# The causal mask of the first attention, added by GpSimd to each head's forget sums

## The reference

```python
def forgetting_attention(q, k, v, log_f):          # 16 heads of 64, Q_BLOCK = 128
    scale = dh ** -0.5
    c = jnp.cumsum(log_f.astype(jnp.float32), axis=1).transpose(0, 2, 1)
    for i in range(S // Q_BLOCK):
        q0 = i * Q_BLOCK
        q1 = q0 + Q_BLOCK
        s = jnp.einsum("bqhd,bkhd->bhqk", q[:, q0:q1], k[:, :q1]).astype(jnp.float32) * scale
        s = s + c[:, :, q0:q1, None] - c[:, :, None, :q1]
        causal = jnp.arange(q0, q1)[:, None] >= jnp.arange(q1)[None, :]
        p = jax.nn.softmax(jnp.where(causal, s, -jnp.inf), axis=-1)
        outs.append(jnp.einsum("bhqk,bkhd->bqhd", p.astype(v.dtype), v[:, :q1]))
```

## Time and profile before

| | |
|---|---|
| median of 3 runs | 2632.52 us (2631.8 to 2633.27) |
| the profiled execution, its own time | 2633.66 us |
| its span in the profile | 2631.9 us, mean granted clock 0.997 |
| PE busy | 2607.0 us, 99% of the span |
| DVE / ACT / POOL busy | 1370.2 / 968.8 / 123.8 us |
| scores of the first attention begin (L565) | 132.4 us |
| its last transposes and products end, inside `aout` | about 228 us |

### The profile page before, as it was taken

How to read it: one execution, slowest core, us unless ns; L and a number is a source line. 1 busy time by engine, 2 the same in 40 slices (tenths; PEclk the granted TensorE clock), 3 DMA queues, 4 the chain that set the end, 5 groups by cost and what they waited for, 6 DMA issues and landing times.

```text
span 2631.9 us, 30728 instructions
## 1 busy us (share of the span) xinstructions
PE 2607.0 (99%) x12322; PEld 2121.4 (81%) x12322; DVE 1370.2 (52%) x2142; ACT 968.8 (37%) x1528; POOL 123.8 (5%) x138
## 2 busy tenths in 40 slices
PE   9999999999999999999998999999999999999999
PEld 7867888888888788888875788888888688888887
DVE  4365763664434776376657544344542365544343
ACT  4265442443226643244445432233223233432221
POOL 0000000000001100000012000000120500000000
PEclk9999999999999999999999999999999999999999
DMA  4311233232232133223320233233332032323222
GB/s 154 126 64 56 90 96 104 96 104 97 96 104 65 43 104 111 81 96 104 95 90 26 73 104 104 86 99 96 104 121 88 9 104 96 97 96 104 91 99 83
DMA packets 66830, 240.49 MB, mean 91 GB/s; under 512 B 7728, under 2 KB 7856, under 8 KB 66560
## 3 DMA queue, kind: packets, MB, share of 16 engines
q1 hardware_dynamic: 63936, 229.38, 26.6%
q0 software_dynamic: 2752, 9.15, 1.1%
HBM read 236.37 MB, written 2.13 MB: 91 GB/s over the span
## 4 chain that ended last, share of the span: by engine, by line
PE 95%; DVE 2%; ACT 2%; issue 1%; POOL 0%; DMA 0%; SPq 0%; DVEq 0%; POOLq 0%; ACTq 0%
PE ps L453 29%; PE ps L454 29%; PE ps L455 29%; PE ps L565 2%; PE ps L585 1%; PE ps L605 1%; PE ps L857 1%; ACT m_B_P L1745 1%; PE ps L844 1%; ACT m_E_P L1745 0%; PE ps L518 0%; PE ps L571 0%; DMA m_x<-in_xT 0%; DVE m_E_P L1018 0%; PE ps L521 0%
## 5 line engine op out<-in xcount | busy, mean ns | idle before, releaser
L453 PE MATMUL ps<-m_xs,m_wsp 128*128 128x512 f32 x2232 | 873.8, 391 | 3.2 <-DVE m_xs L929 3.2
L455 PE MATMUL ps<-m_xs,m_wsp 128*128 128x512 f32 x2232 | 869.1, 389 | 0.0
L454 PE MATMUL ps<-m_xs,m_wsp 128*128 128x512 f32 x2232 | 869.0, 389 | 0.0
L1636 ACT ACTIVATE m_wsp<-m_raw 128x1024 fp32r<-128x1024 f32 (+1 forms) x429 | 446.0, 1051 | 783.3 <-PE ps L455 750.5
L902 DVE TENSOR_TENSOR m_wsp<-m_raw,m_wsp 128x1024 fp32r<-128x1024 f32 (+1 forms) x429 | 516.8, 1221 | 162.6 <-ACT m_wsp L1636 162.3
L453 PEld LDWEIGHTS ps<-m_xs,m_wsp 128*128 128x128 f32 x2232 | 419.4, 188 | 92.5 <-issue 6.1
L454 PEld LDWEIGHTS ps<-m_xs,m_wsp 128*128 128x128 f32 x2232 | 419.5, 188 | 88.0 <-issue 1.7
L455 PEld LDWEIGHTS ps<-m_xs,m_wsp 128*128 128x128 f32 x2232 | 419.4, 188 | 87.2
L955 DVE TENSOR_TENSOR m_x<-m_x,ps 128x512 f32<-128x512 f32 x104 | 71.0, 687 | 316.6 <-PE ps L455 316.6
L453 PE MATMUL ps<-m_wsp,m_xs 128*128 128x512 f32 x320 | 125.7, 393 | 0.0
L455 PE MATMUL ps<-m_wsp,m_xs 128*128 128x512 f32 x320 | 125.1, 391 | 0.0
(11 more groups left out here) (301 smaller groups left out, 3181.8 us busy)
## 6 DMA issues: line engine op xcount, KB each, us to landing
m_raw<-in_w SPq DMA_DIRECT2D x427, 512.0 KB, 3.3
m_A_cb<-csum POOLq DMA_DIRECT2D x16, 256.0 KB, 3.8
m_x<-in_xT SPq DMA_DIRECT2D x4, 512.0 KB, 7.8
m_B_bias<-in_biasB POOLq DMA_DIRECT2D x8, 256.0 KB, 3.1
out<-m_x SPq DMA_DIRECT2D x8, 256.0 KB, 2.0
m_raw<-in_w SPq DMA_DIRECT2D x4, 256.0 KB, 6.9
m_O_D<-in_decay POOLq DMA_DIRECT2D x1, 1024.0 KB, 5.0
m_O_cs<-in_ropeo POOLq DMA_DIRECT2D x1, 512.0 KB, 4.7
```

What stands on the lines that cost most here:

```text
L453: e.matmul(out, lh, rh, start=first, stop=False)
L454: e.matmul(out, lh, rl, start=False, stop=False)
L455: return e.matmul(out, ll, rh, start=False, stop=final)
L1636: e.activation(wsp[n % NSP][:, 0, o:1024], raw[n % NRAW][:, o:1024], ACT.Copy).then_inc(*s_hi(n))
```

## The change

On PE the mask products are gone. In their place the mask is in the row that DVE adds. A buffer of `A_cb` is now 7 blocks of 128 columns wide: the loaded sums stand in blocks 3 to 6, GpSimd adds the fp32 `mask` to copies of key blocks 0, 1 and 2 in blocks 0 to 2, and to key block 3 in place, in block 6. It does this for each of the 16 heads with two instructions (`A_masked`), and DVE's `scored` waits for it (`s_masked`) and no longer for the load itself.

For each query block the masked keys must lie beside plain ones in a way that one instruction of DVE can read. So the key blocks stand in another order: (1, 0) for query block 1, (2, 0, 1) for query block 2. The scores of these two blocks therefore take two products instead of one, first the masked block and then the others. DVE reads the 2 blocks of query block 1 with a step between them. The values are taken in the new order (`kbs`).

```diff
-def causal_units(pairs):
+def causal_units(pairs, orders=((0,), (0, 1), (0, 1, 2), (0, 1, 2, 3))):
...
-            A_cb = ring(c, "A_cb", 6, [128, S])
...
+            A_cb = ring(c, "A_cb", 6, [128, 7 * 128])
...
-                        last = {}
-                        for j in u.jobs:
-                            s = j.segs[si]
-                            last[j] = e.matmul(bank(pre, "score", j.n)[:, s["c0"]:s["c0"] + s["n"]], spec["q"](u, j, s),
-                                               spec["k"](u, j, s), start=True, stop=not spec["more"](j, s))
-                        for j in u.jobs:
-                            s = j.segs[si]
-                            more = spec["more"](j, s)
-                            for ei, (o, n, lt, rh) in enumerate(more):
-                                last[j] = e.matmul(bank(pre, "score", j.n)[:, s["c0"] + o:s["c0"] + o + n], lt, rh,
-                                                   start=False, stop=ei == len(more) - 1)
-                            if s is j.segs[-1]:
+                        for part in zip(*(spec["k"](u, j, j.segs[si]) for j in u.jobs)):
+                            last = {}
+                            for j, (o, n, keys) in zip(u.jobs, part):
+                                s = j.segs[si]
+                                last[j] = e.matmul(bank(pre, "score", j.n)[:, s["c0"] + o:s["c0"] + o + n],
+                                                   spec["q"](u, j, s), keys, start=True, stop=True)
...
-                k=lambda u, j, s: A_k[64 * j.par:64 * j.par + 64, u.p, 0:s["n"]],
-                more=lambda j, s: [(s["n"] - 128, 128, identb[:, :], maskb[:, :])],
+                k=A_keys,
...
-                biased=lambda u, j: d_cb[j.h % 6]["cb", j.h]))
...
+                P=A_P, st=A_st, among=nothing, out=out_split("A"), bias=A_bias, biased=lambda u, j: s_masked[j.h]))
...
-            for h in range(16):
+            def A_sums(h):
                 if h >= 6:
                     q.wait_ge(*s_top["A", A_units[3 * ((h - 6) // 2) + 2].jobs[-1].n])
-                load(A_cb[h % 6][:, :], a["csum"][h:h + 1, :].broadcast_to([128, S]), d_cb[h % 6], ("cb", h))
+                load(A_cb[h % 6][:, 384:896], a["csum"][h:h + 1, :].broadcast_to([128, S]), d_cb[h % 6], ("cb", h))
+
+            def A_masked(h):
+                cb = A_cb[h % 6]
+                q.wait_ge(*d_mk["mk"])
+                q.wait_ge(*d_cb[h % 6]["cb", h])
+                three, one = (mask[:, :].rearrange("p (b n) -> p b n", b=1).broadcast_to([128, 3, 128]), mask[:, :])
+                e.tensor_tensor(cb[:, 0:384].rearrange("p (b n) -> p b n", b=3),
+                                cb[:, 384:768].rearrange("p (b n) -> p b n", b=3), three, ALU.add)
+                e.tensor_tensor(cb[:, 768:896], cb[:, 768:896], one, ALU.add).then_inc(*s_masked(h))
+
+            for h in range(6):
+                A_sums(h)
+            for h in range(16):
+                A_masked(h)
+                if h % 2 and h < 11:
+                    A_sums(h + 5)
+                    A_sums(h + 6)
```

More of the change, by code:

```diff
@@ L9 @@
 F32R = mybir.dt.float32r
-BF16 = mybir.dt.bfloat16
-U16 = mybir.dt.uint16
 ALU = mybir.AluOpType
@@ L198, in causal_units @@
                     n = 128 * (qb + 1)
-                    segs.append(dict(c0=c0, n=n, qb=qb, kbs=range(qb + 1), oc=128 * qb))
+                    segs.append(dict(c0=c0, n=n, qb=qb, kbs=orders[qb], oc=128 * qb))
                     c0 += n
@@ L267, in build @@
         ident = sb(ctx, "ident", [128, 128])
-        identb = sb(ctx, "identb", [128, 128], BF16)
-        maskb = sb(ctx, "maskb", [128, 128], BF16)
+        mask = sb(ctx, "mask", [128, 128])
         ones = sb(ctx, "ones", [128, 128])
@@ L397, in bank @@
             return ps[bank_of.get(key, 0)]
-        d_cf, d_id, d_idb, d_mk = (sem(f"d_{n}", 16) for n in ("cf", "id", "idb", "mk"))
+        d_cf, d_id, d_mk = (sem(f"d_{n}", 16) for n in ("cf", "id", "mk"))
         d_x = [sem(f"d_x{i}", 16) for i in range(4)]
@@ L1016, in scored @@
                             sc = bank(pre, "score", j.n)[:, s["c0"]:s["c0"] + s["n"]]
+                            to = P[j.n % len(P)][:, s["c0"]:s["c0"] + s["n"]]
+                            if pre == "A" and s["qb"] == 1:
+                                sc, to = (t.rearrange("p (b n) -> p b n", b=2) for t in (sc, to))
                             q.wait_ge(*spec["biased"](u, j))
                             i = e.tensor_tensor_reduce(
-                                out=P[j.n % len(P)][:, s["c0"]:s["c0"] + s["n"]], in0=sc, in1=spec["bias"](u, j, s),
+                                out=to, in0=sc, in1=spec["bias"](u, j, s),
                                 scale=-1.0, scalar=3.0e38, op0=ALU.add, op1=ALU.min, accum_out=mx[:, si:si + 1])
@@ L1162, in vector_program, with A_bias @@
             over(ST["ain"], ain)
+            def A_bias(u, j, s):
+                cb = A_cb[j.h % 6]
+                if s["qb"] == 1:
+                    return cb[:, 128:640].rearrange("p (b t n) -> p b t n", b=2, t=2)[:, :, 0, :]
+                return cb[:, {0: slice(0, 128), 2: slice(256, 640), 3: slice(384, 896)}[s["qb"]]]
             scored, loop = attention("A", A_units, dict(
-                P=A_P, st=A_st, among=nothing, out=out_split("A"), bias=lambda u, j, s: A_cb[j.h % 6][:, 0:s["n"]],
-                biased=lambda u, j: d_cb[j.h % 6]["cb", j.h]))
+                P=A_P, st=A_st, among=nothing, out=out_split("A"), bias=A_bias, biased=lambda u, j: s_masked[j.h]))
             over(ST["av"], rows_out(ST["av"], A_v, rc("mix0"), s_col["mix0"]),
@@ L2107, in gpsimd_program @@
             load(ident[:, :], a["ident"], d_id, "id")
-            load(identb[:, :].bitcast(U16), a["identb"], d_idb, "idb")
-            load(maskb[:, :].bitcast(U16), a["maskb"], d_mk, "mk")
+            load(mask[:, :], a["mask"], d_mk, "mk")
             e.memset(A_onr[:, :], 1.0).then_inc(*s_zero("A"))
@@ L2271, in host_consts @@
     o = {}
-    def bits(v):
-        return (np.ascontiguousarray(v).view(np.uint32) >> 16).astype(np.uint16)
     o["ident"] = np.eye(128, dtype=f)
-    o["identb"] = bits(np.eye(128, dtype=f))
     i = np.arange(128)
-    o["maskb"] = bits(np.where(i[:, None] >= i[None, :], 0.0, NEG).astype(f))
+    o["mask"] = np.where(i[:, None] >= i[None, :], 0.0, NEG).astype(f)
     m = np.zeros((128, S), f)
```

28 lines of the change are left out of this document (18 added, 10 removed).

## The result

After the change the median is 2645.41 us (four runs, 2644.66 to 2649.98), beside 2632.19 us for the kernel before (four runs). The medians differ by 13.2 us. The ratio, taken over all runs, is 1.0053, 95% interval 1.0037 to 1.0069: slower by 13.9 us, at least 9.7. The forecast said about 2641 us, between 2636.0 and 2645.5. The median lies just inside that range; by the ratio the kernel stands at 1.0053 x 2632.52 = 2646.5 us, 1 us above it. The profiled execution took 2644.66 us, its span is 2642.8 us.

The account below looks back on a forecast made before the run. PE, busy 99% of the span, was taken as the bound. -8.4 saved, +13.0 stalls, +1.1 given back make +5.7; with +2.7 for the clock, 2633.66 becomes 2642.1, so the median about 2641 us, range 2636.0 to 2645.5.

Parts of the forecast that it names:

- What PE saves: PE's rounds in the first attention get 1.05 us shorter without mask products, to 8.05; eight rounds save 8.4 us.
- the gain arrives: Rival: masks come within the old slack, so PE's saving shows, less about 1.8 us given back: 2625.9 us, chance 0.08.
- What GpSimd costs: GpSimd's two mask additions take 1.40 us per head, between 1.28 and about 1.55.
- the copy's rate: Rival: GpSimd adds about as fast as it copies, 0.75 us per head: 2631.7 us, chance 0.12.
- a slower addition: Rival: GpSimd needs from 1.7 us per head because of the mask's repeated blocks: 2644 to 2646 us, chance 0.07.
- The stall: Masks queued behind POOL's waiting loads make five rounds 10.6 us, PE idle some 2.6 us in each: 13.0 us.
- What went back at the start of the loop: PE reaches the loop earlier but waits there for probabilities and copies, giving back 1.1 us.
- The clock: PE's clock falls behind its new waits, costing 0.55 us a round, 2.7 us in all; bounds 0 and 10.5 us.
- DVE and GpSimd hold each other up: Rival: DVE's scalings wait for additions of heads 12 to 15, losing 1.5 us: 2642.5 us, chance 0.05.

Follow-up runs that it names:

- e4: The changed kernel without GpSimd's mask additions in the first attention, DVE reading the loaded sums as they are: 2626.01 us, ratio 0.9974.
- e7: The changed kernel with masks added ahead, each head's additions behind their loads waiting until a unit's scalings are done: 2625.39 us, ratio 0.9977.
- e6: The changed kernel, masks of heads 12 to 15 waiting for unit 14's scalings, plus nine PE products of ones before some units' transposes: 2638.88 us, ratio 1.0027.
- e2: The changed kernel with the masks of heads 12 to 15 waiting until DVE has scaled unit 14: 2642.99 us, ratio 1.0037.
- e3: The changed kernel with nine PE products of ones before the transposes of units 2, 5, 8, 11 and 14: 2644.04 us, ratio 1.0047.
- e5: The changed kernel with POOL waiting for its own last addition before each of heads 12 to 15: 2642.43 us, ratio 1.0037.
- e1: The changed kernel with POOL's list reordered, masks put ahead of the loads that wait for DVE: 2628.87 us, ratio 0.9989.
- e9: The kernel before, plus eight GpSimd additions in a row into an unread tile behind unit 15's last scores: 2633.17 us, ratio 1.0006.
- e10: The changed kernel with one pause in POOL's additions, only before head 12: 2639.65 us, one run.
- e11: The changed kernel with pauses in POOL's additions only before heads 13, 14 and 15: 2640.82 us, one run.

## Why the forecast had the sign and missed the size

**What PE saves: right.** In e4 PE's entries for units 3p, 3p+1 and 3p+2 are shorter by 0.62, 0.20 and 0.21 us, 1.03 a round for the forecast's 1.05. The round itself is 8.17 to 8.20 and not 8.05: PE waits some 0.15 us in each. The rival "the gain arrives" gave 2625.9 us; e4 took 2626.01 and e7 2625.39. So this gain was there, and all of it was lost to the order on POOL.

**What GpSimd costs: right.** 1.37 to 1.38 us a head for 1.40. The rivals with the copy's rate and with a slower addition fall. The Trainium skill, GPSIMD Engine Reference, section "Performance versus the Vector engine", has about 2.6 cycles for each element, from which 1.11 us for the pair, before any dispatch, is an estimate; the trace has 0.27 us more, and decides.

**The stall: right in place, a little small.** Loads, mask, mask, DVE, ACT, PE came in the predicted order, and the first round after took 10.61 us for 10.6. What went back at the start of the loop was 0.44 + 1.21 us for the 0.23 + 0.58 of the earlier trace rows, 0.84 us. The forecast's sum has 1.1 here, though its own working (0.62 + 0.21) gives 0.83. The waits of DVE are as said for the odd head (0.71 for 0.8); for the even head its idle time is 2.2 us, of which the forecast's 1.1 counted only what is left once the scores are there. With the low clock and the long hold taken away the loss is 7.3 us (e6) for 5.7. 1.1 of the difference are one round of 9.11 us that was taken for 8.05, most of it four scalings that meet additions; 0.3 are another round, of 10.9. The rest is below what the runs can tell.

**The clock: right in kind, and in size as far as the runs can tell.** The forecast had 2.7 us, a quarter of its upper bound. What the nine products gain is 2.6 us by the ratios (1.0037 - 1.0027, e2 against e6; 3.8 by the medians) where the hold is gone, and 1.6 us (e3 against the kernel after; 1.1 by the medians) where it is there. Each ratio has an interval of 0.1% or more to either side, so the close agreement with 2.7 is partly luck. The traces say the same: beside the same rounds of e6 (10.91 and 10.64 us) those from 169.12 and from 180.69 us are 0.7 and 1.6 us longer in the kernel after. Which stalls the low clock follows changes from one execution to the next. In the profile of the kernel after it follows four of five. In that of e5 it follows one (181 to 185 us, granted clock 0.57), and the rounds lose 0.95 us by it. In that of e2 the four rounds together lose 4.3 us. The five runs of e2 show it too: the two with a mean clock of 0.997 took 2640.63 and 2641.39 us, the three with 0.995 2642.99 to 2643.40. So it may be a part of why the runs of the kernel after lie between 2644.66 us (0.995) and 2649.98 us (0.993).

**The step that failed: DVE and GpSimd hold each other up.** It stood as a rival at 1.5 us with a chance of 0.05, and at nothing in the sum, "about the longer addition once or twice". One scaling was held for 3.9 us over six additions. Two traces give what that cost PE. The rounds of e3 with the hold and behind it take 13.19 and 9.97 us, those of e6 10.64 and 9.11: 3.4 us more. In the kernel after they take 13.73 and 10.42, 4.4 us more, with a lower clock in them. By the ratios the hold is 4.2 us, the kernel after against e2 (2.1 by the medians). The profiled executions of the kernel after and of e6 differ by 6.7 us. The four rounds behind the first take 47.95 us and 41.30, so 6.65 us of it lie there: 0.7 and 1.6 in two rounds with a low clock, 4.4 in the two with the hold.

With 7.3 us for e6, 2.6 for the clock and 4.2 for the hold one comes back to the 13.9 measured (14.1, by rounding and by mixing medians with ratios). That agreement proves nothing, since the three are differences along one chain of kernels. The evidence lies in the rows: which scaling is held, and which round is longer by it. Without the hold, by e2 and e5, the kernel would have taken 1.0037 x 2632.5 = 2642.3 us, within the range. The place was named (the run of heads 12 to 15), and the price was not worked out for the case in which a scaling doesn't get its turn at the first boundary: from its arrival at 202.20 the run goes on for 4.7 us, and that was the upper bound to take. The reason given for the low chance, that no row shows the two together, was a reason for a wide bound and not for a small one.

The Trainium skill, SBUF — State Buffer, section "Who interferes with whom", says that a `tensor_scalar` in its two-port mode and a GpSimd instruction lock each other out for a whole instruction, whoever issues first. e1, e9, e10 and e11 agree with it: a scaling of 0.28 us takes up to 1.03 in e1, one of 0.48 takes 1.25 in e9, and additions get longer as well. The 4.40 us of the kernel after are more than the page's one instruction, and there the measurement decides.

**Left open.** Why the scaling in the kernel after and in e3 is passed over for six additions in a row. It starts within 0.01 us of a short addition in both. But nearness to a short addition is not enough: in e1 scalings of 256 columns start 0.04 to 0.05 us behind one, in a run without pause, and are over in 0.56 us. e10 and e11 bound it (another moment or a pause ends it); no run here shows what decides. The cost of the clock could be had to 1 us only with many more runs.

## What to carry to other kernels

Work that is handed to an idle engine stands in that engine's list behind whatever it waits for: look there first, and put work whose inputs are ready ahead of anything in that list that has to wait for another engine. Here this order alone was the difference between 2645.4 and 2628.9 us. Where DVE scales and GpSimd adds in the same stretch, let each addition start from the end of the scalings, as e7 does, and price a run of k additions beside a scaling at up to the length of the run. PE loses twice by a stall here: the stall itself, and in some rounds the low clock behind it. To price the two apart, run the kernel once with PE kept at work through the stalls, as e3 and e6 do.

## What was not expected of the hardware

- A scaling of 512 columns was recorded with 4.40 us beside a run of GpSimd additions without pause, for 0.48 alone, and two with 5.01 in a second kernel (e3); with the same start and a pause behind the first addition, 0.73 (e11).
- The loss goes both ways: additions of 128 and 384 columns took 0.69 and 1.18 us in e10 where scalings went in between, for 0.45 and 0.99.
- Idle times of PE of 2.5 to 2.6 us were followed by a low clock in some rounds and not in others of the same execution: in the kernel after the clock is 1.00 from 158 to 162 us, behind 2.60 us of idle time, and 0.57 from 170 to 174, behind 2.51.
